# Loading the cached keys of the sample attention one sample ahead of the values

## The reference

```python
def fox_sample(q, k, v, logf, cache_k, cache_v, cache_logf, page_table):
    k_all = jnp.concatenate([cache_k[page_table].reshape(db, past, N_HEADS, HEAD_DIM).astype(k.dtype), k], axis=1)
    v_all = jnp.concatenate([cache_v[page_table].reshape(db, past, N_HEADS, HEAD_DIM).astype(v.dtype), v], axis=1)
    ...
    sc = jnp.einsum('bqhd,bkhd->bhqk', q, k_all).astype(jnp.float32) * scale
    bias = ft[:, :, past:, None] - ft[:, :, None, :]
    p = jax.nn.softmax(jnp.where(mask, sc + bias, -jnp.inf), axis=-1)
    return jnp.einsum('bhqk,bkhd->bqhd', p.astype(v_all.dtype), v_all)
```

## Time and profile before

| | |
|---|---|
| median of 3 runs | 1669.56 us (1664.97 to 1670.01) |
| the profiled execution, its own time | 1671.55 us |
| span of the profiled execution | 1669.4 us |
| mean granted TensorE clock over the span | 0.91 of full |
| TensorE (PE) busy | 1492.2 us, 89% of the span |
| VectorE (DVE), ScalarE (ACT) busy | 380.6 us, 222.3 us |
| moved by DMA | 482.00 MB, mean 289 GB/s |

### The profile page before, as it was taken

How to read it: one execution, slowest core, us unless ns; L and a number is a source line. 1 busy time by engine, 2 the same in 40 slices (tenths; PEclk the granted TensorE clock), 3 DMA queues, 4 the chain that set the end, 5 groups by cost and what they waited for, 6 DMA issues and landing times.

```text
span 1669.4 us, 16591 instructions
## 1 busy us (share of the span) xinstructions
PE 1492.2 (89%) x6509; PEld 716.9 (43%) x6509; DVE 380.6 (23%) x728; ACT 222.3 (13%) x428; POOL 20.7 (1%) x45
## 2 busy tenths in 40 slices
PE   6887899979966858999999999999999999999994
PEld 2655566645544635344333333333433433333432
DVE  2100242653221152111102111121120120120114
ACT  2010104212222010101001100100100100100111
POOL 1000000000000100000000000000000000000000
PEclk9898999965587975999999999999999999999996
DMA  8537542400044610899999999999999999999970
GB/s 288 190 106 260 207 178 101 172 34 1 26 139 139 255 51 6 313 401 416 415 419 416 416 418 419 415 417 419 415 416 421 415 415 418 417 416 418 418 311 32
DMA packets 110319, 482.00 MB, mean 289 GB/s; under 512 B 12089, under 2 KB 12577, under 8 KB 77476
## 3 DMA queue, kind: packets, MB, share of 16 engines
q1 hardware_dynamic: 108804, 476.38, 71.5%
q0 software_dynamic: 1440, 4.49, 0.8%
HBM read 476.75 MB, written 4.10 MB: 288 GB/s over the span
## 4 chain that ended last, share of the span: by engine, by line
PE 70%; DMA 19%; SPq 5%; DVE 3%; issue 2%; ACT 1%; POOL 0%; ACTq 0%; PEldq 0%; DVEq 0%; POOLq 0%
PE bank L1358 30%; DMA ring<-in_w_gate_up_dram 15%; PE bank L1136 12%; PE bank L1331 7%; PE bank L1035 5%; PE bank L1352 3%; PE bank L1293 2%; SPq L352 2%; PE bank L1175 2%; PE bank L1176 2%; DMA ring<-in_cache_k_dram 2%; PE bank L1068 1%; DMA ring<-in_w_ada_dram 1%; PE bank L1193 1%; SPq L267 1%
## 5 line engine op out<-in xcount | busy, mean ns | idle before, releaser
L1358 PE MATMUL bank<-ring,work 128*64 128x512 f32 x2048 | 463.1, 604 | 17.6 <-issue 10.9
L1358 PEld LDWEIGHTS bank<-ring,work 128*64 128x64 f32 x2048 | 157.9, 138 | 291.7 <-issue 275.5
L1358 PE MATMUL bank<-ring,hT 128*64 128x512 f32 x1024 | 233.2, 597 | 17.9 <-DMA ring<-in_w_gate_up_dram 16.6
L1136 PE MATMUL bank<-hT,ring 128*128 128x320 f32 x768 | 214.7, 440 | 21.2 <-DMA ring<-in_w_in_dram 13.8
L1015 DVE TENSOR_TENSOR gbT<-gbT,bank 128x320 f32<-128x320 f32 x136 | 66.3, 487 | 518.2 <-PE bank L1352 514.8
L1136 PEld LDWEIGHTS bank<-hT,ring 128*128 128x128 f32 x768 | 147.0, 193 | 86.1 <-issue 23.9
L1358 PEld LDWEIGHTS bank<-ring,hT 128*64 128x64 f32 x1024 | 70.8, 136 | 160.0 <-issue 118.5
L1331 PE MATMUL bank<-qT,tok 128*128 128x256 f32 (+1 forms) x432 | 134.4, 443 | 2.3 <-DVE qT L947 2.3
L1331 PEld LDWEIGHTS bank<-qT,tok 128*128 128x128 f32 (+1 forms) x432 | 75.6, 202 | 66.5 <-issue 59.2
L1352 PE MATMUL bank<-work 128*128 128x320 f32 x272 | 93.9, 471 | 3.2 <-issue 3.2
L984 DVE TENSOR_SCALAR work<-bank 128x512 f32<-128x512 f32 x32 | 21.9, 686 | 271.1 <-PE bank L1358 271.1
(11 more groups left out here) (272 smaller groups left out, 889.1 us busy)
## 6 DMA issues: line engine op xcount, KB each, us to landing
ring<-in_w_gate_up_dram SPq DMA_DIRECT2D x128, 2048.0 KB, 21.5
ring<-in_w_down_dram SPq DMA_DIRECT2D x128, 1024.0 KB, 19.6
ring<-in_w_ada_dram SPq DMA_DIRECT2D x12, 2048.0 KB, 9.1
ring<-in_w_in_dram SPq DMA_DIRECT2D x12, 2048.0 KB, 12.0
ring<-in_cache_k_dram SPq DMA_DIRECT2D x16, 512.0 KB, 5.0
ring<-in_cache_v_dram SPq DMA_DIRECT2D x16, 512.0 KB, 4.5
ring<-in_w_out_dram SPq DMA_DIRECT2D x2, 2048.0 KB, 8.2
out_dram<-work POOLq DMA_DIRECT2D x2, 1024.0 KB, 6.8
```

What stands on the lines that cost most here:

```text
L1136: last = mm(ps[:, 0:T], w[:, k, 128 * (t % 4):128 * (t % 4) + 128], hT[:, k, :], start=(k == 0), stop=(k == NT - 1))
L1358: last = mm(bank[CAP * x:CAP * x + CAP, :], lhsT[:, CAP * x:CAP * x + CAP], rhs(x), start=start, stop=stop)
```

## The change

SyncE issues the same 32 transfers in another order. Before, it issued for each sample its two pages of keys and then its two pages of values. Now it issues the keys of samples 0 and 1 first, and then for each sample b the values of b and the keys of b + 2. Each group keeps the wait that it had. Nothing else of the program is changed.

```diff
-            for b in range(DB):
-                for g, c, in_ in ((0, cache_k, k_in), (NPG, cache_v, v_in)):
-                    if b >= 2 and g == 0:
-                        eng.wait_ge(s["KT_ps"], 4 * (b - 1))
-                    if b >= 2 and g:
-                        eng.wait_ge(s["sy_ps"], b - 1)
-                    for i in range(NPG):
-                        eng.dma_start(kv[:, b % 2, g + i, :],
-                                      c[0, ds(page(eng, NPG * b + i), 1), :, :, :].rearrange("o p h d -> (o p) (h d)"))\
-                            .then_inc(in_[b % 2], 16)
+            def cached(b, g, c, in_):
+                for i in range(NPG):
+                    eng.dma_start(kv[:, b % 2, g + i, :],
+                                  c[0, ds(page(eng, NPG * b + i), 1), :, :, :].rearrange("o p h d -> (o p) (h d)"))\
+                        .then_inc(in_[b % 2], 16)
+
+            def keys_in(b):
+                if b >= 2:
+                    eng.wait_ge(s["KT_ps"], 4 * (b - 1))
+                cached(b, 0, cache_k, k_in)
+
+            def values_in(b):
+                if b >= 2:
+                    eng.wait_ge(s["sy_ps"], b - 1)
+                cached(b, NPG, cache_v, v_in)
+
+            keys_in(0)
+            keys_in(1)
             for b in range(DB):
-                ...
+                values_in(b)
+                if b + 2 < DB:
+                    keys_in(b + 2)
```

## The result

| | before | after |
|---|---|---|
| median, same comparison | 1668.26 us (4 runs, 1664.97 to 1670.01) | 1641.51 us (4 runs, 1639.05 to 1643.8) |
| ratio | | 0.9841, 95% interval 0.9826 to 0.9855 |
| profiled execution, its span | 1669.4 us | 1639.7 us |
| five iterations that wait for keys before | 68.77 us | 40.12 us |

The kernel became 26.75 us faster, 1.6%. The prediction was 1641 us.

What follows compares the result with a forecast made beforehand. TensorE waits for cached keys queued behind values in SyncE's program. Five iterations save 68.77 - 5 x 8.02 = 28.7 us; 1671.55 - 28.7 = 1642.9, with the median 2.0 lower: 1641 us, range 1634 to 1650.

Steps and rivals of the forecast that it cites:

- The wait for keys: Sample attention, iterations 1 to 5: all five TensorE waits for keys go, 4.33 us in iteration 1; slack 3.6 us each.
- The clock behind the wait: Key transposes and fold after the wait: half clock costs 1.29 us in iteration 1; whole iteration difference taken, 28.7 us.
- Does 8.02 us repeat?: Samples' loop: later iterations also take 8.02 us; neither SyncE's issues (3.6 us) nor transfers (5.0 us) become the period.
- The values of sample 1: Start of the samples: issued later, there at 463.8, used at 470.03; cover 6.2 us, cost nothing.
- The change without effect: SyncE's queue: keys still behind the fold that they waited for; 1670 us, 2 in 100.
- a part of the wait stays: Samples' loop: transfers land later, 3 us of wait stays in each of five iterations; gain 14, 1655 us; 6 in 100.
- Transposes at the half clock even without a wait: Key transposes: each of five iterations still pays 1.29 us, 6.5 us in all; 1647.5 us; 10 in 100.
- The loop held at the half clock: Samples' stretch to the merge: TensorE's busy time doubles, 12.3 us slower, 1682 us; 2 in 100 slower, 1 a draw.
- The last two iterations: End of the samples' loop: they load no keys, so their 10.48 us to the merge stay.
- Behind the samples: Merge to end: shift passed on; half-clock stretches priced at nothing, at most 2.75 and 13.4 us back at full clock.

Runs made afterwards that it cites:

- the filler: Kernel before, old order, plus 14 matmuls that nobody reads ahead of the key transposes of samples 3 to 7; 1660.26 us, ratio 0.9949.
- keys held back a little: Changed kernel, keys of samples 3 to 7 also wait for svalues of the iteration that issues them; 1639.23 us, ratio 0.9823 to the kernel before.
- the last version: Changed kernel, half the key transposes moved before svalues, values waiting for svalues(b - 2) instead of its fold; 1630.63 us, ratio 0.9764 to the kernel before.
- the sixth experiment: Changed kernel, but values of sample 1 keep their old place at the start, ahead of the first wait; 1638.95 us, ratio 0.9827 to the kernel before.
- the split: Changed kernel, first two of four key transpose groups of sample b + 2 moved between sweights(b) and svalues(b); 1634.6 us, ratio 0.9797 to the kernel before.
- the weaker wait: Kernel before, old order, values of sample b wait for svalues of sample b - 2 and no longer for its fold; 1647.21 us, ratio 0.9871.
- keys held back further: Changed kernel, keys of samples 3 to 7 also wait for the key transposes of the sample ahead; 1646.87 us, ratio 0.988 to the kernel before.

## Why the prediction was right

*The wait for keys.* All five waits went, by the mechanism that was named. The two experiments that held keys back, by 3.1 and some 5.6 us, put the slack where the working had it, at 3.6 us with a landing of 5.49 us.

*The clock behind the wait.* Expected 1.29 us an iteration; the filler gives 5.96 / 5 = 1.19. The 28.65 us had a third part, about 1 us, most of it half clock at the start of the last of the five. Taking the whole difference between iteration 0 and the later ones, and not the wait alone, was the step that made the sum right: by the wait alone it would have been 21.7 us.

*Does 8.02 us repeat?* It did, to a hundredth, in both profiled executions of the changed kernel and in two variants of it (keys held back a little, early values). Neither SyncE's issues nor the DMA engines became the period; the last version moves the same pages every 6.71 us.

*The values of sample 1* cost nothing, as the sixth experiment shows. *The change without effect* and *a part of the wait stays* are refuted by the list of waits.

*Transposes at the half clock even without a wait.* Refuted: five iterations of the change at 1.00 throughout, 16 transpose instructions in each. The rule of the Trainium skill that was weighed (TensorE: Matmul & The Clock Gate, Part 4: PE-mode transpose) does not hold for this loop, in which transposes share each iteration with matmuls. *The loop held at the half clock* did not occur either; the rows of the five iterations and the ratio exclude it.

*The last two iterations* were priced at no change and cost 1.74 us in the profiled execution. It is a fall of the clock (0.79 in place of 1.00), and where it comes from stays open. The changed kernel took 12.26 us in both of its profiled executions, and so did the version with the early values of sample 1; the first with keys held back, the filler and the split took 10.5 us as before, and the remaining ones 11.6 to 12.7. So the fall is not tied to the new order: the weaker wait, in the old order, has it too, with 12.66 us. In the changed kernel no idle time above 0.78 us stands ahead of it. No experiment was aimed at it. It is the one term of the sum that came out otherwise than it was priced.

*Behind the samples* the shift was passed on to 0.10 us. The stretches at the half clock that might have changed did not. The gathering answers to its row:

```profile
611.00:639.70 28.70, 26.54 (x53) 13.90 (x55) 5.01 (x11) 2.24 (x4) 0.00 (x0) 0.50 0.00 0
```

The forecast of 28.7 us lies between the two measurements of the changed kernel, 26.75 us in the first comparison and 32.8 in the last. Its agreement with 1641.51 to half a microsecond is luck and closer than such a sum can promise: the forecast started from a median of 1669.56 where the comparison had 1668.26, and took off 28.7 where 26.75 was measured, and the two differences offset each other in part; two comparisons of the same pair of kernels differ by 6 us.

## What to carry to other kernels

A queue that is issued in order passes each wait on to all that stands behind it. For every transfer, ask which wait it needs and which it merely inherits, and put transfers with early conditions ahead of those with late ones; weakening the late condition to the last reader of the buffer works too. Alone it took 20.5 of the 28.65 us of the loop, and on top of the new order it had something to add once the split had used up the slack (33.53 us for 38.13); on the change alone, which has no wait left, it was not tried. Look for an iteration in the trace that happens to have its data: it prices the whole loop without the wait, the slower clock behind the wait included. When a loop has become dense, each shortening moves the point at which data are wanted, so reckon the slack again, and with the longest landing seen, not the usual one.

## What the runs showed of the hardware

The clock fell behind short idle times, and not behind all of them. Idle times of 0.75 to 1.1 us, five in a row, left the five iterations at 1.00 (keys held back further). One of 1.75 us was followed by transposes of 3.44 us where 2.5 is usual (weaker wait), one of 1.69 us by eight instructions in 1.97 us where 1.09 is usual (split); one of 2.50 us with filler ahead of it was followed by 1.09. In the last two iterations of the changed kernel, where no idle time is above 0.78 us, 16 instructions of `svalues` took 1.93 us where 1.07 is usual. Which idle times cost the clock cannot be read off their length.

The opposite also occurs. The attention of the prompt is dense and yet at the half clock throughout, in both kernels; this is the changed one:

```profile
375.00:446.00 71.00, 69.00 (x176) 36.78 (x175) 25.06 (x77) 17.17 (x57) 0.00 (x0) 0.50 0.00 1
```

Busy 69.00 of 71 us at 0.50. Together with the gathering that is some 95 busy microseconds of TensorE at half speed; by an estimate, half of it, 48 us, would be the most that a full clock gives back, more than this change had to win. Why the clock does not rise there was not tried.
